# Two of eight channel tiles of a causal depthwise convolution moved from VectorE to GpSimd, in a Trainium2 kernel of transformer blocks

## What is computed

```
z = rms_norm_2(x, g) @ w_in        # q, k, v of the attention, glu_in, two gates
u, gate = split(glu_in + b_glu)
u = u * sigmoid(gate)
u = causal_depthwise_conv(u, w_dw, width=31) + b_dw     # one weight per channel and tap
u = silu(layer_norm(u)) @ w_conv_out + b_conv_out
s = q @ k.T * Dh**-0.5 + bias      # per group and head, bias from a table of distances
o = softmax(s) @ v                 # merged over the 3 groups
```

## Time and profile before

| what | value |
|---|---|
| median of 3 runs | 4051.91 us |
| lowest and highest | 4049.54, 4061.95 us |
| span of the profiled execution, first to last instruction | 4047.0 us |
| TensorE busy | 3733.2 us, 92% |
| VectorE, ScalarE, GpSimd busy | 1956.9, 1577.2, 182.8 us |
| mean granted TensorE clock | 0.930 |

### The profile page before, as it was taken

How to read it: one execution, slowest core, us unless ns; L and a number is a source line. 1 busy time by engine, 2 the same in 40 slices (tenths; PEclk the granted TensorE clock), 3 DMA queues, 4 the chain that set the end, 5 groups by cost and what they waited for, 6 DMA issues and landing times.

```text
span 4047.0 us, 47316 instructions
## 1 busy us (share of the span) xinstructions
PE 3733.2 (92%) x16820; PEld 2963.0 (73%) x16820; DVE 1956.9 (48%) x3245; ACT 1577.2 (39%) x2325; POOL 182.8 (5%) x172
## 2 busy tenths in 40 slices
PE   7999977789999999999868899999999998988998
PEld 5887864458788878887745478788788876866886
DVE  4443454644444434433545555444349773444443
ACT  4432255563444334322355543343232332423431
POOL 1000000000100000000000000000100001010000
PEclk9999987789999999999867799999999996988999
DMA  3223230012232322233210023223322210222231
GB/s 120 98 99 104 92 107 1 1 39 101 83 99 96 101 89 96 99 106 102 84 40 1 0 99 99 89 96 101 108 89 94 67 62 16 94 78 73 93 104 68
DMA packets 88727, 322.27 MB, mean 80 GB/s; under 512 B 10591, under 2 KB 10847, under 8 KB 88472
## 3 DMA queue, kind: packets, MB, share of 16 engines
q1 hardware_dynamic: 83952, 304.35, 22.7%
q0 software_dynamic: 3840, 13.17, 0.9%
q10 hardware_dynamic: 808, 3.07, 0.2%
HBM read 318.40 MB, written 10.02 MB: 81 GB/s over the span
## 4 chain that ended last, share of the span: by engine, by line
PE 86%; DVE 7%; ACT 5%; issue 2%; ACTq 0%; DVEq 0%; POOLq 0%; POOL 0%; DMA 0%
PE bank L254 24%; PE bank L256 24%; PE bank L255 24%; PE bank L911 2%; PE bank L1315 2%; PE bank L1342 1%; PE bank L901 1%; PE bank L889 1%; PE bank L1331 1%; DVE val L1448 1%; ACT prob_t L1006 1%; DVE h_lo L336 1%; DVE sq L1125 1%; DVE ssq L1074 1%; PE bank L528 1%
## 5 line engine op out<-in xcount | busy, mean ns | idle before, releaser
L250 DVE TENSOR_TENSOR unit_lo<-unit_raw,unit_hi 128x1024 fp32r<-128x1024 f32 x572 | 702.5, 1230 | 881.2 <-ACT unit_hi L245 870.0
L254 PE MATMUL bank<-h_hi,unit_hi 128*128 128x512 f32 x2688 | 1063.0, 395 | 15.2 <-DVE unit_lo L250 11.7
L255 PE MATMUL bank<-h_lo,unit_hi 128*128 128x512 f32 x2688 | 1054.8, 392 | 0.0
L256 PE MATMUL bank<-h_hi,unit_lo 128*128 128x512 f32 x2688 | 1054.5, 392 | 0.0
L245 ACT ACTIVATE unit_hi<-unit_raw 128x1024 fp32r<-128x1024 f32 x572 | 601.1, 1052 | 406.9 <-PE bank L256 395.6
L254 PEld LDWEIGHTS bank<-h_hi,unit_hi 128*128 128x128 f32 x2688 | 510.9, 190 | 125.2 <-DVE unit_lo L250 13.4
L255 PEld LDWEIGHTS bank<-h_lo,unit_hi 128*128 128x128 f32 x2688 | 510.5, 190 | 107.5 <-issue 1.7
L256 PEld LDWEIGHTS bank<-h_hi,unit_lo 128*128 128x128 f32 x2688 | 510.0, 190 | 107.8
L254 PE MATMUL bank<-act_hi,unit_hi 128*128 128x512 f32 x880 | 346.7, 394 | 0.0
L256 PE MATMUL bank<-act_hi,unit_lo 128*128 128x512 f32 x880 | 345.0, 392 | 0.0
L255 PE MATMUL bank<-act_lo,unit_hi 128*128 128x512 f32 x880 | 341.5, 388 | 0.0
(11 more groups left out here) (268 smaller groups left out, 4478.0 us busy)
## 6 DMA issues: line engine op xcount, KB each, us to landing
unit_raw<-in_units SPq DMA_DIRECT2D x572, 512.0 KB, 3.3
bias_rows<-bias_once POOLq DMA_DIRECT2D x2, 3840.0 KB, 16.2
bias_t<-bias_rows POOLq DMA_DIRECT2D x16, 256.0 KB, 3.0
x<-in_x SPq DMA_DIRECT2D x1, 2048.0 KB, 10.0
out_x<-x SPq DMA_DIRECT2D x8, 256.0 KB, 2.1
mixer_gains<-in_mixer_gains ACTq DMA_DIRECT2D x2, 736.0 KB, 5.4
mixer_constants<-in_mixer_constants ACTq DMA_DIRECT2D x2, 560.0 KB, 4.2
bias_t<-bias_rows POOLq DMA_DIRECT2D x8, 128.0 KB, 2.4
```

Source lines behind the costliest of these rows:

```text
L250: nc.vector.tensor_tensor(w_lo[u % SLOTS][:], raw[u % SLOTS][:], w_hi[u % SLOTS][:].bitcast(F32), ALU.subtract).then_inc(unit_lo, 1)
L254: nc.tensor.matmul(out_ap, w_h, r_h, start=first, stop=False)
L255: nc.tensor.matmul(out_ap, w_h, r_l, start=False, stop=False)
L256: return nc.tensor.matmul(out_ap, w_l, r_h, start=False, stop=last)
```

## The change

GpSimd computes the channel tiles 6 and 7, VectorE the first six. [...] 12 taps stand ahead of the wait for the transfers of h = 2, 9 ahead of each of h = 3 to 7, and the last 5 behind them.

```diff
+    conv_sum, conv_tap = sq
...
+    DVE_TILES = 6
...
     def blk1_dve(dve, f, r):
-        taps = [(c, k) for c in range(KD) for k in range(CW)]
+        taps = [(c, k) for c in range(DVE_TILES) for k in range(CW)]
...
     def blk1_pool(pool, f):
         fence(pool, f)
         pool.wait_ge(bias_stored, 16 * L)
+        taps = [(c, k) for c in range(DVE_TILES, KD) for k in range(CW)]
+        at, steps = [0], [0]
+
+        def step(ins):
+            steps[0] += 1
+            ins.then_inc(s["conv_p"], 1)
+            pool.wait_ge(s["conv_p"], steps[0])
+
+        def convolve(count):
+            for c, k in taps[at[0]:at[0] + count]:
+                u0 = c * CU
+                w = bc("w_dw", c * CW + k)
+                if k == 0:
+                    pool.wait_ge(s["glu"], KD)
+                    step(nc.gpsimd.tensor_scalar(conv_sum[:], u_conv[:, u0:u0 + S], w, bc("b_dw", c), ALU.mult, ALU.add))
+                else:
+                    dst = conv_sum[:] if k < CW - 1 else u_conv[:, u0 + CW - 1:u0 + CU]
+                    step(nc.gpsimd.tensor_scalar(conv_tap[:], u_conv[:, u0 + k:u0 + k + S], w, None, ALU.mult))
+                    step(nc.gpsimd.tensor_tensor(dst, conv_sum[:], conv_tap[:], ALU.add))
+            at[0] += count
+
         for h in range(NH2):
             if h >= 2:
+                convolve(12 if h == 2 else 9)
                 pool.wait_ge(s["job_red"], 4 * (h - 1))
...
+        convolve(len(taps) - at[0])
```

More of the change, by code:

```diff
@@ L216, in program @@
     s = {}
-    for n in ("gains_in bias_tab_in bias_mm bias_out_a bias_out_v glu qk_out o_out conv job_parts mean centred c_norm c_val c_hi c_lo ya_out x_post y_norm "
+    for n in ("gains_in bias_tab_in bias_mm bias_out_a bias_out_v glu qk_out o_out conv conv_p job_parts mean centred c_norm c_val c_hi c_lo ya_out x_post y_norm "
               "stat_sum stat_std stat_rs stat_diag rstd h_f32 h_hi h_lo "
```

## The result

| | before | changed |
|---|---|---|
| median, us (4 runs each) | 4056.42 (4049.54 to 4061.95) | 4088.31 (4079.83 to 4089.77) |
| ratio | | 1.007, 95% interval 1.0053 to 1.0088 |
| span of the profiled execution | 4047.0 | 4088.2 |

The change costs 0.7%: slower, as forecast. The medians of the table differ by 31.9 us; against the 4060.3 us of 23 later runs of the kernel before the difference is 28.0 us, half of the 56 us that were forecast.

What follows compares the result with a forecast made beforehand. VectorE was taken to bound block 2's dense stretch, 3091.5 to 3131.5, with TensorE nearly gapless until 3322. 22.6 + 35.8 - 2.4 = +56.0 us on the 4047.0 span gave 4103.0, plus 4.9 the forecast 4108 us; range 4066 to 4140.

Steps and rivals of the forecast that it cites:

- What is removed: 62 taps, 46.6 us of VectorE's work; gain only 2.4 us, 0.9 at the tail's start, 1.5 behind the last output.
- What is added: 122 GpSimd instructions; first batch 35.4 us, later ones 27.6, transfers at most some 2 us late, costing nothing by durations alone.
- The price of an add: Each GpSimd add beside VectorE's taps in a dense stretch costs VectorE 0.84 us.
- The price of a multiply: Each GpSimd multiply costs VectorE 1.11 us, taken as a longer add, between 0 and 1.57.
- (a): Dense stretch, from 3091.5, the last glu write: GpSimd's first batch of 23 instructions costs 22.6 us, all on the path.
- (b): 3149.8 to 3176.8: 14 meetings, 13.7 us, less two thirds of VectorE's idle time, leaves 7.9 us.
- (e): 3241.9 to 3259.5, where the taps soon end: some 10 GpSimd instructions, 7.2 us after two thirds of idle time.
- only adds exclude: Rival, chance 0.12: multiplies cost VectorE nothing, meetings elsewhere go mostly into idle time; +12 us, 4064 us.
- (d): 3214.8 to 3241.9: 15 meetings, 14.7 us, less two thirds of VectorE's idle time, leaves 9.0 us.
- (c): 3176.8 to 3214.8: 18 GpSimd instructions, 17.6 us, less two thirds of VectorE's idle time, leaves 11.7 us.
- The clock rival: Rival, chance 0.18: TensorE's granted clock falls too, +27 us over 3149.8 to 3259.5, 4135 us.
- likeliest case: Both GpSimd adds and multiplies exclude VectorE's instructions; chance 0.62, range 4082 to 4132 us.

Runs made afterwards that it cites:

- late_start: Changed kernel without GpSimd's first batch of 12 taps ahead of the third head's bias transfer, 17 taps left for the tail: 4070.88 us, ratio 1.0016.
- the relieved kernels: Two VectorE taps per first-pair slot instead of three: changed kernel (all four pairs, GpSimd's first batch moved later) 4057.55 us; kernel before, without GpSimd, 4061.04 us.
- no_gpsimd: Changed kernel with GpSimd's part of the convolution left out, VectorE keeping its six tiles: 4058.12 us, ratio 0.9998 to the kernel before.
- late_two_taps: Changed kernel without GpSimd's first batch of 12 taps, and two VectorE taps per slot of the four pairs instead of three: 4057.55 us, ratio 0.9989.
- adds_only: Changed kernel with each GpSimd multiply replaced by an add of two SBUF tiles, number and order of instructions kept: 4118.49 us (one run).

## Why the prediction was right in direction and too high by 28 us

- **What bounds the kernel**: right. The dense stretch is VectorE's, late_start gives back there all that the change cost there, and the relieved kernels show TensorE's 36.2 us below it.
- **What is removed**, -2.4: the start of the tail gives 1.0 where 0.9 was reckoned, the two taps behind the last output 1.5, and no_gpsimd lies 2.2 us under the kernel before.
- **What is added**: the durations of GpSimd were taken without their meetings. The multiply has 1.88 in the median of 60 and up to 3.02, so the first batch took 45.6 us and not 35.4, and later transfers went up to 8 us after their release. That cost nothing, as forecast, since the tile is needed four jobs later.

```profile
L1533 POOL TENSOR_SCALAR sq<-u_conv,block_columns x60: 1563/1883/3020, 3106.0 to 3369.0; 128x512 f32<-128x512 f32 x60
```

- **The price of an add**, 0.84: right, 0.91 measured.
- **The price of a multiply**, 1.11: the step that failed. "I take it as an add that is 0.27 longer", between 0 and 1.57. It is 0.31 beside a two-input tap. Put into (a), 12 x 0.31 + 11 x 0.91 gives 13.7 us where I had 22.6 and 14.0 was measured. With the mean of the two, 0.61, in place of 0.98 my sum for (b) to (e) comes to 14.8 us instead of 35.8, and 15.8 was measured. The whole sum would be +26 us, against 28 measured: this one term carries nearly the whole error. The rival "only adds exclude" (4064 us, of 12 in 100) was nearer to the mechanism than my case, but took the multiply at nothing and half of the meetings elsewhere as hidden.
- **(b) and (d)**, 7.9 and 9.0: 0.1 and 1.0 measured. Here not the price alone failed but the count of one meeting for each two-input instruction and the two thirds of idle time. VectorE's busy time rose by under 3 us in (b), for 17 instructions of GpSimd, and its idle time took nearly all of it.
- **(c)**, 11.7: 7.0 measured, 5.9 of it between job 7 and job 8. **(e)**, 7.2: 7.7 measured, up to job 19, again 6.1 of it in the empty slots. I spread the cost over whole stretches; it stands in two places of 20 us where VectorE is 80% busy and TensorE has no gap to lend. One price and one share of idle time for stretches of unlike density made (b) and (d) too dear and, at the measured price, (c) and (e) too cheap. That these errors cancel in the sum is luck.
- **The clock rival**: TensorE's granted clock does fall behind each new wait (0.82 from 3230.4 to 3233.0, 0.53 from 3303.6 to 3306.5), and a part of the 0.9, 1.1 and 1.7 us by which the stretches behind the waits are longer will be that. It is under 4 us in all, not 27.
- **The time**: 4088.3 lies in the range, 4066 to 4140, and also in the 4082 to 4132 of the likeliest case, whose condition, that a multiply excludes VectorE as an add does, the runs refute. The 20 us between it and the 4108 forecast are less than the 28 of the cost because the forecast was added to the first three runs, 8 us under the later median. That part is luck too.
- **What would show it**: the mean of the taps in the dense stretch, 1.077, was near the 1.1 expected, although the price was wrong: 39 taps among 11 adds at 0.91 and 11 multiplies at 0.31 are 1.09. What told the difference was the length of the stretch, 54.5 and not 63. The adds' median over the phase, 1.31, says little for "above 1.30"; in the dense stretch 11 of them take 16.4 us, 1.49 each. The reductions stayed as before, as forecast. Splits of 2 us and more came only outside the dense stretch, up to 2.31 us.

## What to carry to other kernels

Handing work from VectorE to GpSimd costs VectorE more than it saves wherever VectorE is already the engine that ends last: here 23 instructions took 14 us from it, and the 62 taps saved 2 to 3, since they were taken off where VectorE had room. Look for the densest 20 us, not for the mean of a stretch. Started behind the densest stretch, GpSimd's work still cost 7.4 and 6.0 us in the next two pairs (late_start); with one tap less in each slot as well it cost nothing that could be measured (late_two_taps). Price a meeting by the kind of GpSimd's instruction and not by its length: the longer multiply cost a third of the shorter add, and a memset nothing.

## What was not expected of the hardware

- A multiply by a column on GpSimd (1.57 us alone) costs a two-input VectorE instruction 0.31 us and a one-input one 0.61, an add (1.26 alone) 0.91 in both cases.
- The same multiply with a second column added in one instruction takes 0.76 us alone on GpSimd, half of the plain multiply. Whether the 60 plain multiplies would be shorter and cheaper in that form was not run.
- In the changed kernel the splits of the dense stretch stay at 1.21 us beside GpSimd's alternating instructions while the taps grow to 1.08; in adds_only the same splits take 1.65. The rhythm of the two engines seems to decide which instructions are hit; no run was made on that.
- One step of the tail, from job 28 to 29, takes 9.9 us in one profile and 11.6 in thirteen, whatever VectorE and GpSimd do. The last step of the phase, from the last maximum to the last output, takes 11.3 to 11.7 us in three and 13.4 in the others, with no order that follows the work. A microsecond or two in the tail should not be put down to the kernel on the strength of one profile; why these steps switch stays open.
